# The first block's output projection on rounded halves, and the second layer's scan without scores for the context

## What is computed

```
# end of the first block; ya, yb are 2048 x 512
outs, lses = zip(*[dilated_attention(qh, kh, vh, w, d) for (w, d) in DILATED_PATTERNS])   # three patterns
wts = softmax(stack(lses))                     # weights of the three patterns
yb  = rms_norm(sum_p wts_p * outs_p * silu(gb), norm_att)
mix = concatenate([ya, yb], -1) @ w_out        # 2048 x 1024 @ 1024 x 1024
x   = x + gate * rms_norm(mix, norm_post)
...
# the scan of the second block, for d in (forward, backward)
s_ctx, oc = hgrn_scan(context part, s0 = 0,     with_output = need_ctx)
_,     ol = hgrn_scan(latent part,  s0 = s_ctx, with_output = True)
# need_ctx is true in the first layer and false in the second
```

## Time and profile before

| quantity | value |
|---|---|
| median of three runs | 5659.86 us (5658.45 to 5660.29) |
| the profiled execution's own time | 5654.59 us |
| its span, first to last instruction | 5652.2 us |
| granted TensorE clock, mean | 0.947 |
| busy: PE / PEld | 4974.5 / 3406.5 us |
| busy: DVE / ACT / POOL | 2412.2 / 1588.9 / 1133.0 us |

### The profile page before, as it was taken

How to read it: one execution, slowest core, us unless ns; L and a number is a source line. 1 busy time by engine, 2 the same in 40 slices (tenths; PEclk the granted TensorE clock), 3 DMA queues, 4 the chain that set the end, 5 groups by cost and what they waited for, 6 DMA issues and landing times. The chain is left out here.

```text
span 5652.2 us, 67843 instructions
## 1 busy us (share of the span) xinstructions
PE 4974.5 (88%) x26717; PEld 3406.5 (60%) x26717; DVE 2412.2 (43%) x4905; ACT 1588.9 (28%) x3017; POOL 1133.0 (20%) x1207
## 2 busy tenths in 40 slices
PE   4888998999686998799999988969988899999889
PEld 2336887877334865583454476758656645544767
DVE  3230022544554465753543046334556645520554
ACT  2231101544124411222333133134111224421331
POOL 1000011000001011143775000010221428860000
PEclk8998999999897999899999999979999899999999
DMA  4001102233432000010000110330000100001112
GB/s 177 5 11 42 53 26 79 84 102 94 153 116 91 23 1 9 1 53 17 12 10 20 51 45 25 114 123 16 9 9 1 49 17 10 12 16 58 45 64 93
DMA packets 155901, 273.43 MB, mean 48 GB/s; under 512 B 12444, under 2 KB 91588, under 8 KB 154948
## 3 DMA queue, kind: packets, MB, share of 16 engines
q1 hardware_dynamic: 143204, 254.42, 13.2%
q10 hardware_dynamic: 12384, 14.68, 0.7%
HBM read 204.12 MB, written 64.95 MB: 48 GB/s over the span
## 5 line engine op out<-in xcount | busy, mean ns | idle before, releaser
L2225 POOL TENSOR_TENSOR y_t<-y_t,weight_ring 128x512 f32<-128x512 f32 x352 | 446.7, 1290 | 73.2 <-ACT weight_ring L2195 68.6
L2243 DVE TENSOR_REDUCE y_t<-ps_max 128x2 f32<-128x1024 f32 x256 | 313.4, 1224 | 331.8 <-PE ps_max L2052 331.8
L1331 DVE TENSOR_TENSOR features_low<-h_t,features_high 128x1024 fp32r<-128x1024 f32 x260 | 304.0, 1171 | 352.2 <-ACT features_high L1296 351.6
L659 PE MATMUL ps_proj<-weight_ring,h_t 128*128 128x256 f32 x2048 | 448.5, 381 | 2.7 <-PE ps_proj L659 2.2
L659 PEld LDWEIGHTS ps_proj<-weight_ring,h_t 128*128 128x128 f32 x2048 | 388.8, 191 | 57.7 <-issue 5.4
L1268 PE MATMUL ps_proj<-features_high,weights_high 128*128 128x512 f32 (+1 forms) x880 | 345.1, 392 | 59.8 <-DVE features_low L1331 30.5
L1296 ACT ACTIVATE features_high<-h_t 128x1024 fp32r<-128x1024 f32 x260 | 259.7, 1001 | 418.5 <-PE ps_proj L1268 356.6
L1268 PE MATMUL ps_proj<-features_high,weights_low 128*128 128x512 f32 (+1 forms) x880 | 339.6, 386 | 0.0
L1268 PE MATMUL ps_proj<-features_low,weights_high 128*128 128x512 f32 (+1 forms) x880 | 338.8, 385 | 0.0
L1474 PE MATMUL ps_s<-qf,kb 64*128 64x128 f32 x3456 | 251.4, 285 | 62.6 <-DVE scores_t L1642 57.3
L1453 PE MATMUL ps_f<-h_t,weight_ring 128*128 128x512 f32 (+1 forms) x640 | 290.5, 586 | 14.4 <-DVE state L1614 14.4
(11 more groups left out here) (329 smaller groups left out, 8911.0 us busy)
## 6 DMA issues: line engine op xcount, KB each, us to landing
weight_ring<-in_w_in_dram SPq DMA_DIRECT2D x40, 1024.0 KB, 5.9
weight_ring<-in_w_mod_dram SPq DMA_DIRECT2D x48, 512.0 KB, 4.0
x_rows<-h_rows SPq DMA_DIRECT2D x32, 512.0 KB, 6.4
t_rows<-t_rows SPq DMA_DIRECT2D x64, 256.0 KB, 2.7
x_res<-h_rows SPq DMA_DIRECT2D x32, 512.0 KB, 3.2
res<-result SPq DMA_DIRECT2D x48, 264.0 KB, 2.1
res_rows<-res SPq DMA_DIRECT2D x48, 264.0 KB, 3.8
h_t<-v_rows SPq DMA_DIRECT2D x3, 4096.0 KB, 14.2
```

The costliest lines, as they stand in the source:

```text
L659: mm = pe.matmul(ps[u % 4][:, 0:GC], hT[:, k, t * P:(t + 1) * P], w[:, k, :], start=(k == 0), stop=(k == KT - 1))
L1331: dve.tensor_tensor(self.fl[:, s % NB, :, 0:n], self.hT[:, k0:k0 + KS, c0:c0 + n], self.fh[:, s % NB, :, 0:n].bitcast(F32), ALU.subtract). ...
L2225: pool.tensor_tensor(acc[g % 2][:, kv, :], before, pT[s % 3][:, kv, :], ALU.add).then_inc(pa.h, 1)
L2243: ins = dve.tensor_reduce(part[:, g % 2, t, c, :].rearrange("p (v i) -> p v i", v=2)[:, :, i], pM[:, :, 0:n], AXX, ALU.max)
```

## The change

**In `stage_output1`**: `w_out` is loaded in eight pieces of 512 KB by ACT's queue into the weight ring; ACT writes each piece times the gain as a high part `w_out_high`, DVE the rest as `w_out_low`. ACT also rounds `yaT` of a tile to `ya_high` and the turned rows to `yb_high`; POOL forms `ya_low`, DVE `yb_low`. PE issues, for each part, 24 products of halves in place of eight f32 products, in the order part a(v), turn(v+1), part b(v). The two sums of the weighted rows and the product with the gate move from DVE to POOL. DVE's order is weights and weighted rows of tile t, then the end of tile t-2, then `yb_low` of tile t. ACT's order is the exponential and `ya_high`, the square of tile t-2, the copies of part a of tile t-1, the square and the copy of `yb`. `mix` has three buffers. The modulation of the second block is formed inside the loop, at t = 4 and 6, and with fewer waits. The stage gives back its semaphores at its end.

**In `stage_hgrn_scan`**: where `out_ctx` is false (second layer) the context step has no score levels, no kept scores, no `qf` and no outputs; of its phases 0 to 7 only `raise_k` stays. The projection of the next step additionally waits for the gates of the steps before it, which in the other steps the first level has waited for already.

The diff, cut to its core:

```
         @block.gpsimd
         def _(pool):
-            for kind, t in order:
-                c = 1 if kind == "y" else 4
-                pool.wait_ge(pw_in.h, pw_in.at(1 + nth[kind, t]))
-                pool.tensor_tensor(stt[:, t, c + 1:c + 2], stt[:, t, c:c + 1], env.mhalf[:, :], ALU.pow).then_inc(pw.h, 1)
+            for t in range(NT + 2):
+                if t < NT:
+                    pool.wait_ge(yah.h, yah.at(t + 1))
...
+                    pool.tensor_tensor(al[:, t % 2, :, :], yaT[:, :, t * P:(t + 1) * P], ah[:, t % 2, :, :].bitcast(F32), ALU.subtract)\
+                        .then_inc(yal.h, 1)
+                    R = r[:, t % NB, :, :]
+                    pool.wait_ge(rm.h, rm.at(t + 1))
+                    for x in range(2):
+                        pool.tensor_tensor(R[:, 0, 0:o], R[:, 0, 0:o], R[:, 1 + x, 0:o], ALU.add).then_inc(ad.h, 1)
+                        pool.wait_ge(ad.h, ad.at(2 * t + x + 1))
...
+                    pool.tensor_tensor(ybn[:, t % 2, :], R[:, 0, 0:o], gb[:, t % NB, :], ALU.mult).then_inc(yb.h, 1)
+                if t >= 2:
+                    root(stt[:, t - 2, 4:5], stt[:, t - 2, 5:6], inm, t - 1, pwm)
+                if t < NT:
+                    root(stt[:, t, 1:2], stt[:, t, 2:3], iny, t + 1, pwy)
...
         @block.tensor
         def _(pe):
+            def part(v, x, banks, hi, lo, done):
+                for half in range(2):
+                    cols = slice(half * CH, (half + 1) * CH)
+                    for k in range(4):
+                        if v == 0 and half == 0:
+                            pe.wait_ge(wls.h, wls.at(4 * x + k + 1))
+                        for n, (y, w) in enumerate(((hi, whi), (hi, wlo), (lo, whi))):
+                            mm = pe.matmul(banks[half][:, :], y[:, v % 2, k, :], w[:, 4 * x + k, cols],
+                                           start=(k == 0 and n == 0), stop=(k == 3 and n == 2))
+                mm.then_inc(done.h, 1)
...
+            for v in range(NT):
+                pe.wait_ge(yal.h, yal.at(v + 1))
+                if v >= 1:
+                    pe.wait_ge(pa.h, pa.at(2 * v))
+                part(v, 0, pA, ah, al, mma)
...
+                if v + 1 < NT:
+                    turn(v + 1)
+                pe.wait_ge(tcl.h, tcl.at(v + 1))
+                if v >= 2:
+                    pe.wait_ge(pb.h, pb.at(2 * (v - 1)))
+                part(v, 1, pB[v % 2], bh, bl, mmb)
...
         @block.vector
         def _(dve):
             for k in range(KT):
                 g = env.cols("norm_rec", 4) if k < 4 else env.cols("norm_att", 4)
-                ins = dve.tensor_scalar(wo[:, k, :], wo[:, k, :], g[:, k % 4:k % 4 + 1], None, ALU.mult)
+                dve.wait_ge(whs.h, whs.at(k + 1))
+                dve.scalar_tensor_tensor(out=wlo[:, k, :], in0=raw[:, k % 4, :], scalar=g[:, k % 4:k % 4 + 1],
+                                         in1=whi[:, k, :].bitcast(F32), op0=ALU.mult, op1=ALU.subtract).then_inc(wls.h, 1)
...
@@ stage_hgrn_scan
+    off = 0 if out_ctx else 1
+    ups = lambda s: 8 * s - (off if s >= off else 0)
...
+                    if k == 0 and s >= 1:
+                        pe.wait_ge(sg[pr].h, sg[pr].at(2 * s))
...
             def level(s, pr, ph):
                 col, n = steps[s]
+                if s < off:
+                    return
...
             def outputs(s, pr):
                 col, n = steps[s]
+                if s < off:
+                    return
...
+                if ph < 8 and s < off:
+                    if ph == 0:
+                        dve.wait_ge(ready[pr].h, ready[pr].at(2 * s + 2))
+                    elif ph >= 2:
+                        dve.wait_ge(up[pr].h, up[pr].at(ph - 1))
+                        dve.wait_ge(pd[pr].h, pd[pr].at(7 * s + ph - 1))
+                    if ph != 1:
+                        raise_k(s, pr, max(ph - 1, 0)).then_inc(up[pr].h, 1)
+                    continue
```

More of the change, by code:

```diff
@@ L1007, in stage_output1 @@
+        junk = env.sb(ctx, "junk", [P, o + D])
+        ah = env.sb(ctx, "ya_high", [P, 2, 4, P], F32R)
+        al = env.sb(ctx, "ya_low", [P, 2, 4, P], F32R)
+        bh = env.sb(ctx, "yb_high", [P, 2, 4, P], F32R)
+        bl = env.sb(ctx, "yb_low", [P, 2, 4, P], F32R)
+        mix = env.sb(ctx, "mix", [P, NX, D])
         stt = env.sb(ctx, "stats", [P, NT, 8])
@@ new lines, in _ @@
+                if 1 <= t <= NT:
+                    v = t - 1
+                    if v == 0:
+                        act.wait_ge(ra.h, ra.at(1))
+                    act.wait_ge(mma.h, mma.at(v + 1))
+                    if v >= NX:
+                        act.wait_ge(hs[v % NX].h, hs[v % NX].at(16 * (v // NX)))
+                    for half in range(2):
+                        act.activation(mix[:, v % NX, half * CH:(half + 1) * CH], pA[half][:, :], ACT.Copy,
+                                       scale=rst[:, 1, v:v + 1]).then_inc(pa.h, 1)
@@ L1125, in _ @@
+                    act.activation(bh[:, t % 2, :, :], quad(pT[:, :]), ACT.Copy).then_inc(tch.h, 1)
         @block.vector
@@ L1567, in _ @@
                     sigmoids(s + 1, pr)
-                if ph in (6, 7):
+                if ph in (6, 7) and s >= off:
                     keep(s, pr, ph)
```

355 lines of the change are left out of this document (186 added, 169 removed).

## The result

The changed kernel takes 5554.8 us (median of 4 runs, 5548.5 to 5565.8) against 5659.2 for the kernel before (4 runs): a ratio of 0.983, 95% interval 0.981 to 0.985. The forecast was 5571, range 5546 to 5602. The profiled execution of the changed kernel took 5556.1 us with a span of 5554.0.

The account below looks back on a forecast made before the run. The output stage was taken as bound by TensorE's products plus a 1.84 us wait for ACT, the scans by TensorE's full queue in step 0. 5659.9 - 58 (output stage) - 31 (two scans) = 5571 us, range 5546 to 5602.

Parts of the forecast that it names:

- The forecast of 89 for the edits: Whole kernel: 58 us gained in the output stage and 31 us in the two second-layer scans.
- the rival without a hold: Output stage: DVE's small operations slip in between, turn 12.0, 15 us more gain, 5556; chance 12%.
- TensorE's 11.6 us: Output stage: TensorE alone would turn in 11.6 us, 48 records in 10.87 plus transposes of 0.71.
- The turn of 13.0: Output stage: DVE's and POOL's chain per tile, with a hold by `ya_low` and a new root wait, takes 13.0 us.
- the one with a second hold: Output stage: POOL's sums against DVE's next operations, or slower strided reads; turn 14.3, 18 us back, 5590; chance 15%.
- The turn of 13.2: Output stage: by the skill's exclusion rule `ya_low` holds DVE 1.1 to 1.3; turn 13.2, stage gain 55.
- The stage's ends: Output stage: `yb_low` of tile 0 at 25 us, tile 2 at 49; 6.0 from last product to last sum.
- 13.5 to the first score of step 1: Second layer's scans: without the context step's score work, step 1 starts 13.5 us earlier.
- the rival by which POOL paces the scan: Second layer's scans: POOL's bounds and products, not PE's queue, set the pace; 8 us less per scan, 5587; chance 7%.
- 2.7 to 2.9 from there to level 1: Second layer's scans: the stretch after step 1's first score stays nearly the same, 2.7 to 2.9 us.
- after it one score level of the second pair and its outputs are gone, 1.9: Second layer's scans: a 0.65 level and outputs of 0.66 and as much again vanish, 1.9; together 15.4 a scan.
- The slower rival: Output stage: POOL becomes the bound, its four big operations taking 2.38 us each; stage some 140 us longer, 5711; chance 3%.

Follow-up runs that it names:

- gate_dve: Changed kernel with the gating product done by DVE inside its wait for POOL's root, sums left on POOL; 5558.9 us (4 runs).
- no_low: Changed kernel without the third product of each part (lower half of y with upper half of weights), 32 instead of 48 records per tile; 5559.6 us.
- root_first: Changed kernel with POOL's root for mix placed ahead of its gating product; 5559.1 us.
- gate_fill4: Changed kernel, gating product on DVE, second-layer scans' first scored step with all four projection pieces ahead of score levels 1 to 4; 5553.1 us, repeated 5554.6.

## Why the prediction was right or wrong

**The start.** I subtracted from 5659.9, a median of 3 runs. The 36 later runs of the kernel before have medians of 5645 to 5649. From there the same sum gives 5558, within 4 us of both medians of the changed kernel. Of the 104 us of the first comparison 89 come from the edits. Of the other 15 the traces show 9.5, in stages without an edit, and there the clock of the axial stage stands out; why the median of before's first three runs is some 13 above its later medians isn't shown. The forecast of 89 for the edits was right in sum, and of the error of 16 in the time 13 lie in the start. The time alone would have fitted the rival without a hold (5556) better than the forecast; it is the rows that decide.

**TensorE's 11.6 us** was a little low. Records follow each other at 0.233 us in this stage (0.226 in the earlier trace rows), so TensorE alone turns in 11.73, as `gate_dve` shows. That TensorE does not set the turn was right (`no_low`).

**The turn of 13.0** was 12.46. Step by step: weighted rows at 4.61 instead of 4.85, because `ya_low`'s hold cost 0.86 and not 1.0, and consecutive rows of DVE overlap by a tenth; POOL's three operations 4.14 (forecast 4.1); the root behind the gating, the new wait, at its place and size; the long operations 2.55 (2.54); the last step 0.65 instead of 0.85, since the mean of `yb` comes while the sum still runs. The mechanism stands and the term was 4% too large, 6.5 us over the twelve turns. The rival without a hold (12.0) falls by the 1.04 us row, the one with a second hold (14.3) by the part b rows, which take their usual 1.40 beside POOL's sums: they have only one SBUF input.

**The rule.** DVE's small operation with two SBUF inputs came 0.29 us after `ya_low` began and ended 0.05 after it; `root_first` shows the same for the 1024-wide product, `gate_dve` the reverse. By the rule of the Trainium skill, SBUF — State Buffer, section "Who interferes with whom", that the pair of instructions exclude each other for a whole instruction and whoever comes first goes through, the traces agree in all three places, though the one held is each time done 0.1 to 0.2 us before the sum of both durations. In the last fifth of a root it doesn't show: DVE's first 8-wide operation with two SBUF inputs starts 0.43 us into a root of 0.55 and takes 0.16, as without one. The turn of 13.2 that I worked out from the rule was too long because DVE reaches its first two-input operation late, and the rest of POOL's instruction is all that it waits for (0.86 and not 1.1 to 1.3); the remainder are the terms above. The statement of the Trainium skill there that a VectorE instruction with at most one SBUF input, outside the two-port modes, does not contend agrees with the part b rows.

**The stage's ends.** `yb_low` of tile 0 at 26.6 us from the start (forecast 25, range 22 to 29), of tile 2 at 51.7 (49), then 150.9 for twelve turns (158.3, of which the modulation was 1.3 and not 2.3), 32.3 to the last sum (32.1), 3.1 to the next transfer (3.7). Sum 238.0 against 243.0. The ramp's 2.7 too short and the turns' 7.4 too long partly cancel.

**The scans.** 13.5 to the first score of step 1 was right (13.7), and with it the rival by which POOL paces the scan falls; so was 2.7 to 2.9 from there to level 1 (2.98). The step that failed is "after it one score level of the second pair and its outputs are gone, 1.9". They are gone, but of the 17.27 us from level 0 to level 5 that saves only 1.45, as the scans without a slow stretch behind the gap show (15.82), and in the others the lower clock takes 1.64 of it back (17.46). The sum had no term for the clock. A further 0.4 is lost behind level 5; why is open. So a scan gains 13.7 - 0.2 - 0.4 = 13.1, and where the slow stretch lies at the scan's start the total is the same. The clock fell behind a gap that grew from 0.95 to 1.82 because work was taken from TensorE where it waits for DVE; I had looked for a new wait in the gates and found none. 13.1 was inside the bounds (12 to 17), and `gate_fill4`, which has no such fall, reaches 16.0.

**The slower rival** was far off: `ya_low` as fp32r takes 1.28, the sums 1.34 and the gating 1.30, all near the 1.267 of the earlier trace rows, and none has the 2.38 of the 1024-wide form.

## What to carry to other kernels

When work is taken from a full TensorE queue, ask what it covered: here the second pair's scores stood in part where TensorE waited for DVE's copies. Taking them away there brought nothing but a longer gap, and in that order each scan lost some 1.6 us to the lower clock. Such a gap can be given work from further on (`gate_fill4`: 3.0 us a scan in the traces, though not in the median time). When two engines share a turn, place GpSimd's two-input operations beside VectorE operations that read PSUM, not beside those that read two SBUF operands. And before a difference of 1% is explained, look at the granted clock of stages that no edit touched, in more than one trace of each kernel.

## What the runs showed of the hardware that I had not expected

- The granted clock of the same stretch of a stage without an edit differs from execution to execution: 486 us at 0.99, 494 at 0.97, 500 at 0.96.
- Behind a gap of 1.82 us it fell to 1.2 GHz for some 3 us in 15 of 18 scans with the new order. In the other three the same 1.5 us were lost earlier in the scan. Behind a gap of 1.67 us, with the projection pieces placed elsewhere, it did not fall (4 of 4). Whether the length of the gap or the work around it tells these apart was not tried.
- A root on POOL over one column, 0.55 us alone, takes 1.04 beside a DVE product of 0.69 that began 0.06 before it.
- 512-wide fp32r records follow each other at 0.233 us in the output stage (DMA share 0.45 to 0.48, POOL busy half of the time) and at 0.226 in the last stage. Why is open; over 16 tiles it is 5 us.
